# Where the transposed quarters of the normed rows wait in PSUM, in a two-block transformer kernel on one core

## The reference, cut to what matters

```
h  = x
h  = even_layer(h, mem)      # 8 differential heads (A), gated convolution, 4 memory heads (X)
h  = odd_layer(h, mem)       # 12 forgetting heads (C), 4 memory heads (X)
hx = modulate(rms_norm_2(h,   g_pre_mix), shift, scale)
hc = modulate(rms_norm_2(ctx, g_pre_mix), cshift, cscale)
h  = h + gate * rms_norm_2(mix(hx, hc))
h  = h + gate * rms_norm_2(swiglu(modulate(rms_norm_2(h, g_pre_ffn), ...)))
```

## The kernel before, in words

| place | rows, key | after sub | next sub reads |
|---|---|---|---|
| 1 | x, e_norm | start | these rows |
| 2 | mem, e_mem | 11 | other rows (x) |
| 3 | mem, o_mem | 51 | other rows (x) |
| 4 | h, o_norm | 83 | other rows (side) |
| 5 | ctx, ctx_A and ctx_B (bias) | 143 | other rows (x) |
| 6 | h, mix_A and mix_B (bias) | 171 | these rows |
| 7 | h, ffn_A and ffn_B (bias) | 207 | these rows |

## Time and profile before

### The profile page before, as it was taken

The page is one execution under the profiler, slowest core; times in us unless marked ns, Lnnn a source line. Parts: engine busy times, 40 slices in busy tenths (PEclk is TensorE's granted clock), DMA queues, the critical chain, the costliest instruction groups (busy, mean ns, idle before and its releaser), DMA issues.

```text
span 1013.9 us, 14680 instructions
## 1 busy us (share of the span) xinstructions
PE 932.0 (92%) x5582; PEld 809.5 (80%) x5582; DVE 681.4 (67%) x1041; ACT 499.0 (49%) x870; POOL 65.6 (6%) x59
## 2 busy tenths in 40 slices
PE   5999898989999799999987899999899499999996
PEld 4788786989887588989877787776688399999885
DVE  5578888769775458788875765658746447765653
ACT  5464555545444355455555545446634544443441
POOL 0201101000000111001110000100001000000000
PEclk9999998999999899999988999999999789999998
DMA  8544543645573545767673655262223347763741
GB/s 320 168 130 154 192 162 122 213 165 189 186 259 110 173 145 189 269 217 261 217 238 116 208 159 189 76 208 84 85 83 97 112 145 229 250 197 94 270 166 42
DMA packets 91815, 174.59 MB, mean 172 GB/s; under 512 B 6733, under 2 KB 11234, under 8 KB 91746
## 3 DMA queue, kind: packets, MB, share of 16 engines
q1 hardware_dynamic: 89248, 166.79, 49.4%
q0 software_dynamic: 1760, 6.24, 1.9%
q10 hardware_dynamic: 738, 0.61, 0.2%
HBM read 172.56 MB, written 1.06 MB: 171 GB/s over the span
## 4 chain that ended last, share of the span: by engine, by line
PE 48%; issue 24%; DVE 17%; ACT 6%; POOL 2%; DMA 2%; SPq 0%; DVEq 0%; POOLq 0%; ACTq 0%
PE acc L1030 9%; PE acc L1032 9%; PE acc L1031 9%; PE acc L1049 4%; DVE wlo L1664 4%; PE acc L1051 4%; PE acc L1050 4%; POOL small L2149 2%; DVE macc L1902 2%; ACT whi L1350 2%; PE tp L1144 1%; DMA raw<-in_o_w_in 1%; DVE small L1709 1%; DMA raw<-in_e_w_in 1%; DVE g L1715 1%
## 5 line engine op out<-in xcount | busy, mean ns | idle before, releaser
L1664 DVE TENSOR_TENSOR wlo<-raw,whi 128x1024 fp32r<-128x1024 f32 (+2 forms) x278 | 324.1, 1176 | 142.4 <-ACT whi L1350 141.8
L1350 ACT CAST whi<-raw 128x1024 fp32r<-128x1024 f32 (+2 forms) x278 | 277.7, 1012 | 163.2 <-PE acc L1032 89.2
L1049 PE MATMUL acc<-xhi,whi 128*128 128x256 f32 x736 | 216.4, 294 | 12.0 <-DVE slo L1704 5.9
L1051 PE MATMUL acc<-xlo,whi 128*128 128x256 f32 x736 | 210.9, 287 | 0.0
L1050 PE MATMUL acc<-xhi,wlo 128*128 128x256 f32 x736 | 210.8, 286 | 0.0
L1030 PE MATMUL acc<-whi,xhi 128*128 128x512 f32 (+1 forms) x352 | 147.7, 420 | 11.9 <-DVE wlo L1664 3.6
L1049 PEld LDWEIGHTS acc<-xhi,whi 128*128 128x128 f32 x736 | 144.0, 196 | 15.5 <-DVE slo L1704 6.2
L1050 PEld LDWEIGHTS acc<-xhi,wlo 128*128 128x128 f32 x736 | 144.0, 196 | 0.7 <-issue 0.5
L1051 PEld LDWEIGHTS acc<-xlo,whi 128*128 128x128 f32 x736 | 143.7, 195 | 0.0
L1032 PE MATMUL acc<-whi,xlo 128*128 128x512 f32 (+1 forms) x352 | 140.5, 399 | 0.0
L1031 PE MATMUL acc<-wlo,xhi 128*128 128x512 f32 (+1 forms) x352 | 140.2, 398 | 0.0
(11 more groups left out here) (308 smaller groups left out, 1197.1 us busy)
## 6 DMA issues: line engine op xcount, KB each, us to landing
raw<-in_e_w_in SPq DMA_DIRECT2D x56, 512.0 KB, 5.6
raw<-in_o_w_in SPq DMA_DIRECT2D x56, 512.0 KB, 5.5
raw<-in_w_mod SPq DMA_DIRECT2D x48, 512.0 KB, 4.4
raw<-in_w_ffn_in SPq DMA_DIRECT2D x40, 512.0 KB, 4.7
raw<-in_w_in SPq DMA_DIRECT2D x28, 512.0 KB, 3.8
raw<-in_w_ffn_out SPq DMA_DIRECT2D x22, 512.0 KB, 4.2
raw<-in_e_w_out SPq DMA_DIRECT2D x16, 512.0 KB, 4.7
raw<-in_o_w_out SPq DMA_DIRECT2D x16, 512.0 KB, 4.2
```

The lines of the kernel that those rows point to most:

```text
L1049: mm(o, wh, hi, start=a, stop=False, skip_group_check=True)
L1051: last = mm(o, wh, lo, start=False, stop=z, skip_group_check=True)
L1350: nc.scalar.copy(whi[:, s.i % SPLIT_SLOTS, 0:s.nk, 0:n], raw[:, s.raw.i % RAW_SLOTS, s.koff:s.koff + s.nk, 0:n]).then_inc(S["hi_ready"], 1)
L1664: tt(wlo[:, slot, 0:s.nk, 0:n], raw[:, s.raw.i % RAW_SLOTS, s.koff:s.koff + s.nk, 0:n], whi[:, slot, 0:s.nk, 0:n].bitcast(F32), ALU.subtra ...
```

## The change

`transposed` no longer takes pairs of `acc`. Each quarter takes the bank named for it, one of "s0", "s1", "tp" and "o", and uses half of it. `acc_uses` no longer counts these steps; two uses less at each call leave the order of the two pairs as it was.

For main rows (places 1, 4, 6 and 7) the call stands where it stood, with the four quarters in s0, s1, tp and o.

For side rows each quarter is put at a position of its own, at rank 1: at place 2 behind subs 9 to 12, all in tp; at place 3 behind subs 52, 53 (s1), 56 and 57 (s0); at place 5 behind subs 141, 142, 143 (s0) and 144 (s1). At place 3 the load of x into h_res (POOL, L2177) follows the last quarter. At place 5 mod_cols and the call stand ahead of the copy panel (subs 140 to 143) instead of behind it.

```diff
-    def transposed(self, norm, key, scale, bias=None):
-
-        for q in range(4):
+    def transposed(self, norm, key, scale, bias=None, pos=None, banks=("s0", "s1", "tp", "o")):
+
+        def quarter(q):
...
-            if q % 2 == 0:
-                self.next_acc(st, "rt_lo")
-                acc = st.acc
+            st.bank = banks[q]
+            self.uses(st, st.bank, "rt_lo")
+            self.src[key] = st.on["rt_lo"]
+            if then and q == 3:
+                then()
+        then = None
+        for q in range(4):
+            if pos is None:
+                quarter(q)
             else:
-                st.acc, st.free["acc"] = acc, None
-                self.busy[("acc", acc)] = ("rt_lo", st.on["rt_lo"])
-        self.src[key] = st.on["rt_lo"]
+                self.at(pos[q], lambda q=q: quarter(q), 1)
...
     stm = pl.norm_rows("h", "h", ("loaded_h", 16))
+    pl.transposed(stm, "side", ROW["e_mem"], pos=[pl.pos + 5 + q for q in range(4)], banks=("tp",) * 4)
     evs += [pl.panel(W, 1024, CW, "x", "norm", gs=64, dst=("g0", 1)),
             pl.panel(W, 2048, CW, "x", "copy", dst=("g0", 2))]
-    pl.transposed(stm, "side", ROW["e_mem"])
...
-    pl.transposed(stm, "side", ROW["o_mem"])
-    pl.load("x", rows=pl.count["rt_ps"])
+    pl.transposed(stm, "side", ROW["o_mem"], pos=[b - 8, b - 7, b - 4, b - 3], banks=("s1", "s1", "s0", "s0"))(
+        lambda: pl.load("x", rows=pl.count["rt_ps"]))
...
-        evs.append(pl.panel(W, 3072 + CW * g, CW, "x", "copy", dst=(buf, 2)))
         if g == 2:
             assert set(range(4)) <= set(pl.chunks)
             pl.tick(pl.step("mod_cols", which="mix", mod_sb=pl.count["mod_sb"]), "mcol_done")
-            pl.transposed(st, "side", "ctx_A", "ctx_B")
+            pl.transposed(st, "side", "ctx_A", "ctx_B", pos=[pl.pos + 1 + q for q in range(4)], banks=("s0", "s0", "s0", "s1"))
+        evs.append(pl.panel(W, 3072 + CW * g, CW, "x", "copy", dst=(buf, 2)))
...
+        def bank_of(name):
+
+            b = {"s0": spsum[:, 0, :], "s1": spsum[:, 1, :], "tp": tp[:, :], "o": opsum[:, :]}[name]
+            return b.rearrange("p (k t) -> p k t", t=T)
...
             def rows_T(st):
-                wait(st.free["acc"])
+                wait(st.free[st.bank])
```

More of the change, by code:

```diff
@@ L293, in transposed, with after @@
                 st.ready_cols = self.count["mcol_done"]
-            if q % 2 == 0:
-                self.next_acc(st, "rt_lo")
-                acc = st.acc
-            else:
-                st.acc, st.free["acc"] = acc, None
-                self.busy[("acc", acc)] = ("rt_lo", st.on["rt_lo"])
-        self.src[key] = st.on["rt_lo"]
+            st.bank = banks[q]
[7 more added lines that the diff above has]
+                quarter(q)
+            else:
+                self.at(pos[q], lambda q=q: quarter(q), 1)
+        def after(make):
+            nonlocal then
+            then = make
+        return after
     def head(self, h, pos, gap=4):
@@ L1059, in rows_T @@
             def rows_T(st):
-                wait(st.free["acc"])
+                wait(st.free[st.bank])
                 for pair in st.ready:
                     wait(pair)
+                bank = bank_of(st.bank)
                 for k in range(2):
@@ L1065, in rows_T @@
                         kk = 2 * st.q + k
-                        last = tr(acct(st.acc)[:, kk % 4, t * P:(t + 1) * P],
+                        last = tr(bank[:, k, t * P:(t + 1) * P],
                                   rows_of[st.xn][:, t, kk * P:(kk + 1) * P], ident)
@@ L1376, in rows_T @@
                         kk = 2 * st.q + k
-                        last = f(hi[:, k, :], acct(st.acc)[:, kk % 4, :], ACT.Copy, scale=a[:, kk:kk + 1])
+                        last = f(hi[:, k, :], bank_of(st.bank)[:, k, :], ACT.Copy, scale=a[:, kk:kk + 1])
                     last.then_inc(S["rt_hi"], 1)
@@ L1387, in rows_T @@
                         kk = 2 * st.q + k
-                        last = f(dst[:, k, :], acct(st.acc)[:, kk % 4, :], ACT.Identity, scale=a[:, kk:kk + 1],
+                        last = f(dst[:, k, :], bank_of(st.bank)[:, k, :], ACT.Identity, scale=a[:, kk:kk + 1],
                                  bias=b[:, kk:kk + 1])
@@ L1697, in rows_T @@
                     for k in range(2):
-                        last = stt(lo[:, k, :], acct(st.acc)[:, (k0 + k) % 4, :], a[:, k0 + k:k0 + k + 1],
+                        last = stt(lo[:, k, :], bank_of(st.bank)[:, k, :], a[:, k0 + k:k0 + k + 1],
                                    hi[:, k, :].bitcast(F32), ALU.mult, ALU.subtract)
```

## The result

The changed kernel takes 1001.77 us (median of 4 runs, 1000.13 to 1006.72) where the kernel before took 1018.38 (median of 4) on the same chip: ratio 0.985, interval 0.980 to 0.990, which is a gain of 11 to 20 us. The forecast was 1000.5 in a range of 994 to 1010. The profiled executions have spans of 1013.9 and 999.1 us, 14.8 apart; all that follows adds up to this difference.

A forecast was written before the change was run, and what follows sets the result against it. PE was taken to bound the kernel nearly throughout, its matmuls busy 92% of the span. Gains of 0.7 + 1.3 + 3.6 + 1.4 + 5.3 + 3.3 + 1.0 = 16.6 us off the median 1017.25 gave 1000.5, range 994 to 1010.

The forecast's parts named there:

- terms 2, 3 and 4: Gains at places 2, 3 and 4: 1.3 (0.5 to 1.6), 3.6 (2.5 to 4.0), 1.4 us (1.0 to 1.7).
- term 1: Place 1, main rows: first sub starts on quarter 0's rest, not quarter 1's; 0.7 us, between 0 and 0.9.
- Place 3: Side rows o_mem: the 2.67 us wait and the slow stretch behind it go; 3.6 us, between 2.5 and 4.0.
- Place 2: Side rows e_mem: waits of 0.23 and 1.34 us go, one quarter waits 0.3; 1.3 us, between 0.5 and 1.6.
- Place 4: Main rows: the 1.4 us wait goes, since the next panel's pair is free; between 1.0 and 1.7.
- Place 5: Ctx rows: 7.9 us of wait and slow clock go, less new waits; net 5.3 us, between 2.0 and 7.8.
- Place 6: Main rows: wait shortened by 1.8 us, 1.5 left, clock stays up; 3.3 us, between 1.8 and 3.5.
- Place 7: Main rows: quarter 0's rest ends 1.4 us before quarter 1's, partly lost to low clock; 1.0 us, 0.7 to 3.0.
- A: Rival: place 5 brings 1 us instead of 5.3, quarters wait over 2 us and lower the clock; 1004.8 us, 15%.
- C: Rival: later waits for wlo take up what the moves bring; gain under 5, about 1013 us, 8%.
- D: Rival: releases of side quarters' shared banks come late, each also lowering the clock; slower by 9.4, 1026.7 us, 4%.
- B: Rival: short waits at places 2, 3, 5 and 6 lower the clock too; net gain 10.1, 1007 us, 12%.

The follow-up runs named there:

- p3_early: Changed kernel with quarter 2 of place 3 one sub earlier, ahead of the convolution's taps, same banks; 997.63 us, ratio 0.9787 to the kernel before.
- p3_later: Changed kernel with quarters 2 and 3 of place 3 moved behind the convolution's taps, both still in s0; 1000.05 us, ratio 0.9803 to the kernel before.
- p3_bank_o: Changed kernel with quarter 3 of place 3 in bank o instead of s0; 996.63 us, ratio 0.9788 to the kernel before.
- p2_old: Changed kernel with place 2 alone put back into pairs of acc as before; 1005.17 us, ratio 0.9872 to the kernel before.
- side_only: Kernel before with only the side rows (places 2, 3 and 5) changed, main rows as they were; 1014.9 us, ratio 0.9949 to the kernel before.
- passable: Changed kernel with ctx-row quarters no longer pulling the C head's exponentials and scaling ahead of themselves; 1004.83 us, ratio 0.9856 to the kernel before.
- p3_old: Changed kernel with place 3 alone put back into pairs of acc as before; 1003.85 us, ratio 0.9835 to the kernel before.

## Why the prediction was right, and where it wasn't

**The bound and the mechanism** held: PE was the bound at each place, the waits for `rt_lo` behind the transposes went, and the new ones at places 3 and 5 stand where the text put them. The total came out at 14.8 by the traces and 16.6 by the medians, for a forecast of 16.6. But the sum was right partly because its errors cancel: terms 2, 3 and 4 came out beyond their own bounds, and term 1 at its lower one. And part of the agreement is luck, since the interval of the ratio reaches from 11 to 20 us, and at places 1, 6 and 7 single traces of the same form differ by 1.7 to 3.5 us. The forecast itself is off its own sum by 0.15 (1017.25 − 16.6 = 1000.65).

- **Place 3, the step that failed**: "Quarter 3 comes behind the convolution's taps on DVE and may wait some 0.4 us for quarter 2." It waited 2.60, and the low clock behind it took 1.47 more; 3.6 forecast, -0.1 measured, below the term's lower end of 2.5. The text named the taps and then priced the wait by the round trip of place 2, without adding the taps' 4.7 us (L1753, L1757 and L1760 above) to DVE's queue. Shown by p3_early, p3_later and p3_bank_o; the repaired place brings 4.2 in all six traces that have it.
- **Place 2**: 1.3 forecast, 2.0 in all ten traces that have it, above the term's upper end of 1.6. The wait of 0.3 at one of the quarters in tp didn't come: PE passed them at 49.71 and 52.97 with no idle time. The idle time that went is 0.23 + 1.34; the other 0.4 is PE's busy time, which the sum held to be unchanged. Part of the gain may be given back behind sub 29, as p2_old shows.
- **Place 1**: 0.7 forecast, -0.1 in the trace, and yet the mechanism held. Ahead of quarter 0's rest ACT rounds the next weights and DVE splits them, and in the changed kernel's execution those weights landed later. ACT's rounding, first of the kernel before, then of the changed one:

```profile
11.28 1.05 ACT L1350 CAST whi<-raw 128x1024 fp32r<-128x1024 f32 x1 [0.40 <-DMA raw<-in_e_w_in]
```

```profile
11.89 1.05 ACT L1365 CAST whi<-raw 128x1024 fp32r<-128x1024 f32 x1 [0.94 <-DMA raw<-in_e_w_in]
```

  From the end of that rounding to PE's first matmul it is 2.9 us in the kernel before and in side_only, and 2.1 in all twelve traces with the place changed: 0.8 gained each time. The landing took 0.6 of it back here. By sub 3 the twelve traces stand from 0.5 late to 1.7 early, also because part of sub 0 runs at 0.43 us from one matmul to the next instead of 0.23 in seven of them, as in the kernel before, and not in five.
- **Place 4**: 1.4 forecast, 2.5 measured, above the term's 1.7; 2.2 to 2.6 in ten of the twelve traces with it and 3.9 to 4.0 in two. It is 1.6 by the first sub and 0.8 to 0.9 by sub 93. The first part is the wait. The second stands in eleven of the twelve traces and not in side_only, where place 4 is as before: the low clock at sub 89 lasts 6.8 us there and in the kernel before, 3.4 to 3.5 in the twelve. It was not in the sum, and no run took apart why.
- **Place 5**: 5.3 forecast, 4.8 measured, and 4.0 to 4.8 in the eight traces that have it in this form. Quarter 0 waited 5.10, for a forecast of 3.88 + 0.7 = 4.6; quarter 2 waited 1.16, for 1.3, and passable shows that it came from the pulled halves, as forecast. The low clock behind place 5 is gone (1.00 from 526 on).
- **Place 6**: 3.3 forecast, 3.5 measured, with a wait left of 1.96, not 1.5: quarter 0's rest came 1.8 earlier than quarter 1's, as forecast, but the transposes also ended 0.46 earlier against it (1.91 us from the first to the end, for 2.37), 0.23 of which is the wait for L1410 ahead of quarter 2. So the wait did not come under the 1.6, and five of the twelve traces have the low clock behind it and bring 1.8. See below.
- **Place 7**: 1.0 forecast, 2.2 in the stretch. Of this 0.4 stands ahead of the transposes and is not the place's, 1.35 is the wait (2.01 to 0.66) and 0.5 the low clock, which ends 5.1 us behind the first matmul instead of 6.2. So the 1.4 was not halved, and the earlier end of the low clock, the text's reason for its 3.0, came in part. In six of the twelve traces with this form the stretch brings 2.2 to 2.5, in the other six 5.7, beyond the term's 3.0: there the clock is back at 1.00 with the first matmul of the sub. Windows of its first 5 us, changed kernel and p3_bank_o:

```profile
796.28:801.28 5.00, 5.00 (x23) 5.00 (x24) 2.08 (x3) 5.00 (x11) 0.00 (x0) 0.50 0.00 0
```

```profile
794.54:799.54 5.00, 5.00 (x42) 5.00 (x43) 2.08 (x3) 5.00 (x12) 0.00 (x0) 1.00 0.00 0
```

- **+1.6 and -1.5 outside the places**: not in the sum. The first is not the change's: up to sub 9 the same wait of 2.23 stands in both kernels and the clock behind it was 1.00 in the changed one (window 38 to 44) and low in the one before. Behind sub 29 it was the other way round, and there the wait is longer in the changed kernel, 1.38 for 0.65, as in every trace with place 2 changed. Timeline and window of the changed kernel:

```profile
115.99 1.95 PE L1159 MATMUL tp<-cst,macc 128*128 128x1 f32 x16 [1.38 <-DVE macc L1917]
...
118.00:122.00 4.00, 4.00 (x23) 4.00 (x23) 3.57 (x8) 2.33 (x6) 0.70 (x1) 0.59 1.04 393
```

**The rivals.** A fell: place 5 brought 4.8, not 1. C fell: no wait for wlo of the size of the gain. D fell in total, but its mechanism, a shared bank freed late by DVE, is what happened at one quarter of its seven, for 2.60 us and a low clock. The text priced it at 2.2 + 1.5 for each quarter, and that one quarter cost 3.27 + 1.47.

B, and the statement that "waits up to about 1.6 us leave the clock alone", came out mixed. At place 5 the new waits of 1.16 to 1.61 left it at 1.00 in every trace (532 to 540 in the changed kernel). At the mod_out behind sub 29, which the text didn't look at, shorter waits were followed by the lower level: 1.38 in the changed kernel, as just shown, and 1.21 to 1.52 in six others. PE's work there is 16 matmuls of one column, about 2 us long. In p2_old it waited only 0.44, and then (timeline, and windows of p2_old)

```profile
118.10 2.16 PE L1172 MATMUL tp<-cst,macc 128*128 128x1 f32 x16 [0.44 <-DVE macc L1930]
...
120.00:122.00 2.00, 2.00 (x11) 2.00 (x11) 1.56 (x5) 1.97 (x6) 0.70 (x1) 0.50 0.96 364
```

while in p3_old the same mod_out waited 1.18 and the clock stayed:

```profile
117.13 1.95 PE L1172 MATMUL tp<-cst,macc 128*128 128x1 f32 x16 [1.18 <-DVE macc L1930]
...
120.00:122.00 2.00, 2.00 (x20) 2.00 (x19) 1.61 (x5) 1.51 (x3) 0.70 (x1) 1.00 1.05 401
```

So one row at 1.00 behind one wait of 1.61 didn't bear a rule for all waits of that length. The Trainium skill's section that the prediction weighed, "A second HAM failure mode: psum-queue depth-cycling" of "TensorE: Matmul & The Clock Gate", says that brief pauses at PSUM banks can swing the clock. At the new waits for a shared bank the traces agree with it only for the 2.60 at place 3, five times out of five; behind those of 1.16 to 1.61 at place 5 the clock stayed at 1.00 in all ten traces.

## What to carry to other kernels

When a PSUM bank is shared by two producers in a row, price the second one's wait from the queue of the engine that frees the bank: list every instruction that stands ahead of the freeing one in that engine's order, with its duration. The round trip of the freeing work alone is only the lower end. And before a bank is split or added, try to put the freeing instruction ahead of the long block; here one sub earlier brought as much in the trace as another bank (4.2 us).

A wait that is removed is worth its length plus the low clock behind it, and the second part is a draw for waits near 2 us. Two single traces can differ by several us far from the change, so a gain or a give-back seen in a trace should be looked for in several traces and tested by putting that part back and timing it.

## What was not expected of the hardware

The same wait, in the same place of the same order, is sometimes followed by the lower clock level and sometimes not. PE waits 1.96 us at place 6 in every kernel that has its new form. Windows of the 4 us behind it, of the changed kernel and of p3_old:

```profile
624.64:628.64 4.00, 4.00 (x18) 3.33 (x19) 1.38 (x2) 4.00 (x11) 0.00 (x0) 1.00 0.03 11
```

```profile
627.72:631.72 4.00, 4.00 (x12) 3.19 (x13) 1.39 (x2) 4.00 (x11) 0.00 (x0) 0.68 0.04 15
```

18 matmuls in one and 12 in the other. Over the twelve traces with the new form, place 6 brings 3.4 to 3.5 us in seven and 1.8 in five: just the forecast's two ends (1.8 to 3.5), with nothing between. The wait of 1.9 us at the mod_out behind sub 154, which no kernel changes, is followed by 1.00 in five of the fourteen traces and by 0.57 to 0.66 in nine, which costs 1.6 to 1.7 us each time. The wait of 2.16 ahead of sub 206, which no kernel changes either, is followed by 1.00 in six and by 0.57 to 0.69 in eight. Waits of 2.60 and more at the places (2.60, 2.68, 5.10) were followed by the lower level wherever a window was read. With several such spots of 1.5 us in a kernel of 1000, the runs of one kernel spread over 2 to 11 us, which is why gains of 1 to 2 us here could be read in a trace but not told by a median. The outcomes are not independent of each other: the five traces that have the lower level behind place 6 all keep 1.00 behind the 2.16, and of the other seven with the new form six have the lower level there. What decides between the two outcomes of the same wait stays open.
